# A decoder layer with 32 experts: smaller token units over four column groups, whole-row weight loads and a fixed order of experts

## What is computed

```python
def moe(h, w_router, b_router, w_up, b_up, w_down, b_down):
    B, S, D = h.shape
    t = h.reshape(B * S, D)                       # 256 x 1024
    logits = (t @ w_router + b_router).astype(jnp.float32)
    top_vals, top_idx = lax.top_k(logits, TOP_K)  # 4 of 32
    wts = jax.nn.softmax(top_vals, axis=-1)
    combine = jnp.sum(jax.nn.one_hot(top_idx, N_EXPERTS, dtype=jnp.float32) * wts[..., None],
                      axis=1).astype(t.dtype)
    y = jnp.zeros_like(t)
    for e in range(N_EXPERTS):
        gu = t @ w_up[e] + b_up[e]                # w_up[e]: 1024 x 2048
        glu = jnp.minimum(gu[:, 0::2], SWIGLU_LIMIT)
        lin = jnp.clip(gu[:, 1::2], -SWIGLU_LIMIT, SWIGLU_LIMIT)
        act = glu * jax.nn.sigmoid(SWIGLU_ALPHA * glu) * (lin + 1.0)
        y = y + combine[:, e:e + 1] * (act @ w_down[e] + b_down[e])   # w_down[e]: 1024 x 1024
    return y.reshape(B, S, D)
```

## Time and profile before

| | us |
|---|---|
| median of three runs | 1452.26 |
| span of the profiled execution | 1448.6 |
| TensorE busy | 1330.1 (92%) |
| VectorE busy | 396.9 (27%) |
| ScalarE busy | 217.6 (15%) |
| mean DMA rate over the span | 330 GB/s |
| loads of w_up: 256 of 1 MB, issue to landing | 18.0 |
| loads of w_down: 128 of 1 MB, issue to landing | 18.3 |

### The profile page before, as it was taken

One profiled execution on the slowest core, in us unless ns is written; L12 is line 12 of the kernel. 1 busy time (PEld: TensorE's weight loads), 2 busy tenths in 40 slices (PEclk: granted clock), 3 DMA queues, 4 the chain that ended last, 5 costly groups with the idle time before them and its releaser, 6 DMA issues.

```text
span 1448.6 us, 19177 instructions
## 1 busy us (share of the span) xinstructions
PE 1330.1 (92%) x6949; PEld 534.1 (37%) x6950; DVE 396.9 (27%) x1059; ACT 217.6 (15%) x452; POOL 61.9 (4%) x88
## 2 busy tenths in 40 slices
PE   3999999999997999998888989999998988999997
PEld 0484434444444333332222333333333322333332
DVE  0386980654124211211111111121211112112111
ACT  0200102254012111111111111111111111111110
POOL 4000000002532000000000000000000000000000
PEclk9999999999996999999999999999999999999999
DMA  8936666234644899999999999999999999899997
GB/s 273 368 120 249 215 233 216 73 111 124 196 143 142 339 410 409 410 409 409 410 409 409 410 409 409 371 364 410 409 410 410 409 410 410 324 406 410 410 409 310
DMA packets 143057, 477.40 MB, mean 330 GB/s; under 512 B 9746, under 2 KB 9771, under 8 KB 143036
## 3 DMA queue, kind: packets, MB, share of 16 engines
q1 hardware_dynamic: 138918, 472.28, 84.3%
q0 software_dynamic: 1200, 3.28, 0.9%
q10 hardware_dynamic: 2918, 1.57, 0.4%
HBM read 473.96 MB, written 1.05 MB: 328 GB/s over the span
## 4 chain that ended last, share of the span: by engine, by line
PE 48%; SPq 33%; DMA 11%; issue 4%; ACT 2%; DVE 2%; DVEq 0%
SPq L394 28%; PE bank L1155 13%; PE bank L1392 11%; DMA weights<-in_w_up 10%; PE bank L1408 6%; PE bank L1145 4%; PE bank L1166 3%; PE bank L1113 2%; PE bank L1284 2%; PE bank L1367 2%; PE bank L1359 1%; DMA weights<-in_w_ada 1%; SPq L422 1%; SPq L423 1%; SPq L424 1%
## 5 line engine op out<-in xcount | busy, mean ns | idle before, releaser
L1392 PE MATMUL bank<-weights,buf_d 128*64 128x512 f32 x2176 | 504.7, 601 | 48.1 <-DMA weights<-in_w_up 48.0
L1392 PEld LDWEIGHTS bank<-weights,buf_d 128*64 128x64 f32 x2176 | 145.2, 137 | 379.4 <-issue 244.2
L1408 PE MATMUL bank<-weights,buf_d 128*64 128x512 f32 x1088 | 246.7, 595 | 0.0
L1155 PE MATMUL bank<-weights,buf_d 128*128 128x512 f32 x320 | 140.2, 596 | 0.0
L1408 PEld LDWEIGHTS bank<-weights,buf_d 128*64 128x64 f32 x1088 | 74.1, 136 | 125.6 <-issue 117.6
L816 DVE SCALAR_TENSOR_TENSOR weights<-u_conv,convw,weights 128x256 f32<-128x256 f32 x240 | 96.9, 478 | 0.3
L1082 DVE TENSOR_SCALAR u_conv<-bank 128x256 f32<-128x256 f32 x68 | 28.6, 421 | 246.2 <-PE bank L1392 246.2
L1075 DVE TENSOR_SCALAR u_conv<-iota_s,u_conv 128x128 f32<-128x128 f32 x68 | 20.5, 343 | 270.4 <-PE bank L1392 270.4
L1155 PEld LDWEIGHTS bank<-weights,buf_d 128*128 128x128 f32 x320 | 61.2, 192 | 74.3 <-issue 74.0
L683 ACT COPY buf_d<-bank 128x256 f32<-128x256 f32 x68 | 25.3, 373 | 417.5 <-PE bank L1418 417.5
L687 ACT ACTIVATE u_conv<-u_conv 128x256 f32<-128x256 f32 x34 | 14.2, 417 | 385.8 <-DVE u_conv L1082 385.8
(11 more groups left out here) (293 smaller groups left out, 897.3 us busy)
## 6 DMA issues: line engine op xcount, KB each, us to landing
weights<-in_w_up SPq DMA_DIRECT2D x256, 1024.0 KB, 18.0
weights<-in_w_down SPq DMA_DIRECT2D x128, 1024.0 KB, 18.3
weights<-in_w_in SPq DMA_DIRECT2D x14, 2048.0 KB, 11.2
weights<-in_w_ada SPq DMA_DIRECT2D x12, 2048.0 KB, 15.5
weights<-in_w_conv_out SPq DMA_DIRECT2D x2, 2048.0 KB, 7.8
weights<-in_w_attn_out SPq DMA_DIRECT2D x2, 2048.0 KB, 8.2
weights<-in_w_o SPq DMA_DIRECT2D x2, 2048.0 KB, 11.2
qkT<-modrow POOLq DMA_DIRECT2D x16, 128.0 KB, 3.7
```

The source lines that it names most:

```text
L1155: ins = t.matmul(bank(use)[:, :], lhsT[:, k, P * tt:P * tt + P], blk(n)[:, k, :], start=(k == 0 and bias is None), stop=(k == KD - 1))
L1392: ins = t.matmul(UP[a][SLOTS * i:SLOTS * i + SLOTS, :], xgT[:, k, :], wslot(slot, spare_at)[:, k % 2, NB * i:NB * i + NB], start=False, st ...
L1408: ins = t.matmul(DOWN[SLOTS * i:SLOTS * i + SLOTS, :], actT[:, a, k % 2, SLOTS * (k // 2):SLOTS * (k // 2) + SLOTS], wslot(slot)[:, k % 2, ...
```

## The change

- A unit has up to 32 tokens (SLOTS = 32). The moving operand goes over four column groups of 32 columns each: 32 matmuls in `up` write the four quarters of one bank (UP), 16 in `down` those of another (DOWN).
- An expert is loaded in six chunks of 2 MB (CHUNKS). The four chunks of w_up are 256 whole rows of the matrix each; partition p holds rows 2p and 2p+1, 16 KB in one piece. The two chunks of w_down give a partition two pieces of 8 KB. There are seven slots (NSLOT) in a ring over all 192 chunks of all experts.
- The experts run in fixed order, 0 to 31, each at least once; the program text of a unit stands 32 times, each in a loop over that expert's units. Slots, waits and addresses are constants, but for the number of units used up so far (`unit_ends`), which SP and PE read once for each expert. A chunk is loaded into the slot of the chunk seven before it, when PE has used that one in its expert's last unit (`chunk_used[j]`). The first chunk of expert 1 goes out before the routing, into the slot that nothing else holds.
- Because a partition now holds two neighbouring rows, the stationary operands change: `gather` writes the tokens untransposed (32 x 256 in each of four groups, 24 matmuls with 256 columns), ACT copies them, PE transposes even and odd columns apart, ACT copies again (together with the transposed combine weights).
- One activation step for each unit instead of two, on all 128 partitions.
- The routing arithmetic drops the tables of loads, and counts units of 32 (seven comparisons for an expert in place of three).

The core of the diff:

```diff
-SLOTS = 64
+SLOTS = 32
 UCOLS = 64
+GROUPS = P // SLOTS
+CHUNKS = 6
...
-NSLOT = 12
+NSLOT = 7
...
+        def chunk_slot(e, j):
+            return (CHUNKS * e + j) % NSLOT
+
+        def chunk_landed(e, j):
+            return 16 * ((CHUNKS * e + j) // NSLOT + 1)
+
+        def wslot(e, j):
+            at = chunk_slot(e, j)
+            return W[:, at * BLOCKF:(at + 1) * BLOCKF]
+
+        def up_chunk(e, g):
+            return wslot(e, g).rearrange("p (r n) -> p r n", r=2)
+
+        def down_chunk(e, h):
+            return wslot(e, 4 + h).rearrange("p (g r n) -> p g r n", g=2, r=2)
...
-            def load_unit(e, wait, spare=0):
-                for i in range(NSLOT):
-                    wait(i)
-                    pair = 2 * P * (i % 4)
-                    if i < 8:
-                        col = D * (i // 4)
-                        src = w_up[0, e, pair:pair + 2 * P, col:col + D]
-                    else:
-                        src = w_down[0, e, pair:pair + 2 * P, :]
-                    if not isinstance(e, int):
-                        src = src.rearrange("o a n -> (o a) n")
-                    sp.dma_start(wslot(i, spare), src.rearrange("(k p) n -> p k n", p=P)).then_inc(w_full[i], 16)
...
+            def load_chunk(e, j):
+                if j < 4:
+                    src = w_up[0, e, 2 * P * j:2 * P * j + 2 * P, :].rearrange("(p r) n -> p (r n)", r=2)
+                    dst = wslot(e, j)
                 else:
-                    sp.wait_ge(w_free, before * 9 + 3 * (i // 4) + i % 4 + 1)
-
-
-            e1 = sp.value_load(unit_i[0:1, UCOLS + 1:UCOLS + 2], min_val=0, max_val=EXPERTS - 1)
-            before1 = sp.value_load(unit_i[0:1, 2 * UCOLS + 1:2 * UCOLS + 2], min_val=0, max_val=46)
+                    src = w_down[0, e, NB * (j - 4):NB * (j - 4) + NB, :].rearrange("(g p r) n -> p g (r n)", g=2, r=2)
+                    dst = wslot(e, j).rearrange("p (g n) -> p g n", g=2)
+                sp.dma_start(dst, src).then_inc(w_full[chunk_slot(e, j)], 16)
+
+            for j in range(CHUNKS):
+                sp.wait_ge(*used[len(blocks) - RING + j])
+                load_chunk(0, j)
             sp.wait_ge(h2_high, TT)
             sp.wait_ge(h2_split, 3 * (TT - 1) + 1)
-            load_unit(bass.ds(e1, 1), lambda i: slot_used(i, 16, before1), NSLOT * SLOTF)
-            with sp.Fori(2, loads) as n:
-                e = sp.value_load(unit_i[0:1, bass.ds(n + UCOLS, 1)], min_val=0, max_val=EXPERTS - 1)
-                before = sp.value_load(unit_i[0:1, bass.ds(n + 2 * UCOLS, 1)], min_val=0, max_val=46)
-                before_last = sp.value_load(unit_i[0:1, bass.ds(n + (2 * UCOLS - 1), 1)], min_val=0, max_val=46)
-                spare = sp.value_load(load_spare[0:1, bass.ds(n, 1)], min_val=0, max_val=NSLOT * SLOTF)
-                landed = sp.value_load(load_landed[0:1, bass.ds(n, 1)], min_val=16, max_val=16 * EXPERTS)
-                load_unit(bass.ds(e, 1), lambda i: slot_used(i, landed, before, before_last), spare)
+            full(sp, LG_USE[TT - 1])
+            load_chunk(1, 0)
...
+            for e in range(EXPERTS - 1):
+                end = sp.value_load(unit_ends[0:1, e:e + 1], min_val=e + 1, max_val=UCOLS - 1)
+                for j in range(CHUNKS):
+                    n = CHUNKS * e + j + NSLOT
+                    if n < CHUNKS * EXPERTS:
+                        sp.wait_ge(chunk_used[j], end)
+                        load_chunk(n // CHUNKS, n % CHUNKS)
...
+            s.copy(xg, GX[:, 0:T]).then_inc(xs_ready, 1)
+            act_e.wait_ge(xt_done, 1)
+            s.copy(xgT, GX[:, T:2 * T].rearrange("p (r s) -> p r s", r=2)).then_inc(xc_ready, 1)
...
+                act_e.wait_ge(glu_ready, u + 1)
+                s.activation(sg, glu, ACT.Sigmoid, scale=ALPHA).then_inc(sg_ready, 1)
                 act_e.wait_ge(gathered, u + 2)
-                s.copy(xgT, UP[0][:, :].rearrange("p (k s) -> p k s", k=KD)).then_inc(xg_ready, 1)
-                keep_act(1)
-
-                act_e.wait_ge(ct_done, u + 1)
-                s.copy(Cmb, TR[:, 0:T]).then_inc(cmb_ready, 1)
+                s.copy(xg, GX[:, 0:T]).then_inc(xs_ready, 1)
+                act_e.wait_ge(t_done, u + 1)
+                s.copy(actT, TR[:, 0:T].rearrange("p (r s) -> p r s", r=2)).then_inc(actT_ready, 1)
+                act_e.wait_ge(xt_done, u + 2)
+                s.copy(area_q[:, 0:2 * T], GX[:, :]).then_inc(xc_ready, 1)
...
-                for k in range(KD):
-                    for tt in range(TT):
-                        for i, part in enumerate(h2_parts):
-                            ins = t.matmul(UP[0][:, SLOTS * k:SLOTS * k + SLOTS], part[:, tt, P * k:P * k + P],
-                                           pick[:, tt, :], start=(tt == 0 and i == 0), stop=(tt == TT - 1 and i == 2))
+                for tt in range(TT):
+                    for i, part in enumerate(h2_parts):
+                        for g in range(GROUPS):
+                            ins = t.matmul(GX[SLOTS * g:SLOTS * g + SLOTS, 0:T], pick[:, tt, :], part[:, tt, T * g:T * g + T],
+                                           start=(tt == 0 and i == 0), stop=(tt == TT - 1 and i == 2))
                 ins.then_inc(gathered, 1)
+
+            def transpose_halves(bank_, at, src):
+                for r in range(2):
+                    ins = t.transpose(bank_[:, at + P * r:at + P * r + P], src.rearrange("p (c r) -> p r c", r=2)[:, r, :], ident[:])
+                return ins
...
+            def bias_rows(bank_, groups, col):
+                for n_, g in enumerate(groups):
+                    t.matmul(bank_[SLOTS * g:SLOTS * g + SLOTS, :], sel, ebias[:, col + NB * n_:col + NB * n_ + NB],
+                             start=True, stop=False)
...
+            def unit(e, u):
+                pe.wait_ge(xc_ready, u + 1)
                 pe.wait_ge(sel_ready, u + 1)
-                bias(UP[0], 0)
-                with pe.If(spare == 0):
-                    up_chunks(0, range(2 * SPARE))
-                with pe.Else():
-                    up_chunks(0, range(2 * SPARE), NSLOT * SLOTF)
-                up_chunks(0, range(2 * SPARE, KD)).then_inc(up_done[0], 1)
-                bias(UP[1], D)
-                up_chunks(1, range(KD // 2))
+                bias_rows(UP, range(GROUPS), 0)
+                for j in range(4):
+                    w = up_chunk(e, j)
+                    pe.wait_ge(w_full[chunk_slot(e, j)], chunk_landed(e, j))
+                    for r in range(2):
+                        for g in range(GROUPS):
+                            ins = t.matmul(UP[SLOTS * g:SLOTS * g + SLOTS, :], xgT[:, r, SLOTS * j:SLOTS * j + SLOTS],
+                                           w[:, r, NB * g:NB * g + NB], start=False, stop=(j == 3 and r == 1))
+                    ins.then_inc(chunk_used[j], 1)
 
                 pe.wait_ge(oe_ready, u + 1)
-                pe.wait_ge(cmb_ready, u + 1)
                 combine()
-                up_chunks(1, range(KD // 2, KD)).then_inc(up_done[1], 1)
-                pe.wait_ge(act_ready[0], u + 1)
-                transpose_act(0)
+                bias_rows(DOWN, (0, 2), 2 * D)
                 pe.wait_ge(pick_ready, u + 2)
                 gather()
-                pe.wait_ge(actT_ready[0], u + 1)
-                down(0)
-                pe.wait_ge(act_ready[1], u + 1)
-                transpose_act(1)
+                pe.wait_ge(act_ready, u + 1)
+                transpose_halves(TR, 0, act).then_inc(t_done, 1)
+                pe.wait_ge(xs_ready, u + 2)
+                transpose_halves(GX, T, xg)
                 pe.wait_ge(pickw_ready, u + 1)
-                pe.wait_ge(actT_ready[1], u + 1)
                 for tt in range(TT):
-                    ins = t.transpose(TR[:, P * tt:P * tt + P], pickw[:, tt, :], ident[:])
-                ins.then_inc(ct_done, 1)
-                down(1).then_inc(down_done, 1)
-            pe.wait_ge(cmb_ready, count + 1)
-            pe.wait_ge(oe_ready, count + 1)
+                    ins = t.transpose(GX[:, P * tt:P * tt + P], pickw[:, tt, :], ident[:])
+                ins.then_inc(xt_done, 1)
+
+                pe.wait_ge(actT_ready, u + 1)
+                for h in range(2):
+                    w = down_chunk(e, h)
+                    pe.wait_ge(w_full[chunk_slot(e, 4 + h)], chunk_landed(e, 4 + h))
+                    for g in range(2):
+                        at = SLOTS * (2 * h + g)
+                        for i in range(2):
+                            for r in range(2):
+                                rows = slice(SLOTS * (2 * i + r), SLOTS * (2 * i + r) + SLOTS)
+                                ins = t.matmul(DOWN[rows, :], actT[:, r, at:at + SLOTS], w[:, g, r, NB * i:NB * i + NB],
+                                               start=(r == 1 and h == 0 and g == 0), stop=(h == 1 and g == 1))
+                    ins.then_inc(chunk_used[4 + h], 1)
+
+            begin = 0
+            for e in range(EXPERTS):
```

(6 more changed lines are left out.)

199 lines of the change are left out of this document (53 added, 146 removed).

## The result

The changed kernel takes **1479.51 us** (median of four runs, 1477.41 to 1481.32); the kernel before took 1451.28 beside it (1448.71 to 1455.54). The ratio is **1.019**, with a 95% interval of 1.017 to 1.021: slower by 28 us, and within 1 us of the 1480 forecast. The profiled execution has a span of 1475.5 us.

What follows compares the result with a forecast made beforehand. The prediction took the expert stage to be bound by weight loads, TensorE close behind. Start 468.6, chunks 908.4, empty queues 63.3, clock and restart 24, end 12.0 and 3.7 from span to median gave 1480 us; 8-in-10 range 1442 to 1518.

Steps and rivals of the forecast that it cites:

- The sum: Whole kernel: start 468.6, chunks 908.4, empty queues 63.3, clock and restart 24, end 12.0 give span 1476.3; forecast 1480 us.
- experts 15 and 25: Experts with three and four units: the load queue stands empty for 16.9 and 32.4 us, plus clock and restart.
- ten experts with two units: Refill comes late after each repeated unit: 1.4 us lost at each, plus 2 us each for clock and restart.
- the 24 us for clock and restart: At twelve repeated-unit experts: 2 us each for slow DMA restart and TensorE's low clock together; ends 0 and 80.
- The rate: Expert weight loads: longer rows raise the full-queue DMA rate from 410 to 427 GB/s, 4.91 us a chunk; ends 410 and 435.
- The straight line: Load rate extrapolated from 2 and 4 KB rows: 428 GB/s for 8 KB, 438 for 16 KB, 435 mixed.
- rival A: Expert loads: 435 GB/s and no extra at restarts, so 1439 us; chance 0.32 with the cases up to the forecast.
- rival B: Expert loads: long rows load no faster than 4 KB rows, so 1516 us; chance 0.15 with its surroundings.
- The unit: TensorE's work on up to 32 tokens: 15.5 us with four column groups side by side; 25.8 if no faster than two.
- Rival C: TensorE: four column groups run no faster than two, unit 25.8 us, end about 1690; chance 0.05 together with the low-clock case.
- The empty queue: Expert loads: only an expert's last unit frees slots, so twelve repeated experts lose 63.3 us, against 14.9 before.
- Rival D: TensorE: clock stays at 1.2 GHz throughout, unit about 28 us, about 1590; chance 0.05 together with the slow-column-groups case.

## Why the prediction was right, step by step

**The sum.** Its terms against the trace of the changed kernel:

| term | predicted | measured |
|---|---|---|
| engines move again after the start | 468.6 | 467.3 |
| 185 chunks at the plain rate | 908.4 (427 GB/s) | 911 to 913 (426 to 425) |
| experts 15 and 25 | 49.3 + 4 | 50.0 |
| ten experts with two units | 14 + 20 | 33.4 |
| tail behind the last transfer | 12.0 | 10.1 |
| sum | 1476.3 | 1472 to 1474 of a span of 1475.5 |

Some 2 us of the span stand in no term; the first restart, slow for two microseconds like the others (246 and 213 GB/s at 467 to 469), is about one of them. No term is off by more than 5 us; the rate gave less than forecast, start, sags and tail cost less. The mechanisms held; that the total came within 1 us is luck: 427 GB/s was chosen between 410 and 435, and the 24 us for clock and restart between 0 and 80, and the rate's error of 3 to 5 us met about 7 us the other way from start, sags and tail.

**The rate.** TensorE's start on the first and on the last chunk of w_up of expert 31, each behind a wait for the chunk:

```profile
1441.78 2.74 PE L1346 MATMUL bank<-weights,buf_d 128*32 128x512 f32 x16 [2.75 <-DMA weights<-in_w_up]
...
1456.47 3.56 PE L1346 MATMUL bank<-weights,buf_d 128*32 128x512 f32 x16 [2.97 <-DMA weights<-in_w_up]
```

Three chunks of 2.097 MB in 14.69 us are 428 GB/s for rows of 16 KB, and 15 slots of 8 KB rows gave 421 throughout. The packets of the trace agree: they are whole rows, and one of 16 KB takes 612 ns and one of 8 KB 312 (medians), which is 428 and 420 on 16 engines. The straight line had 438 and 428. So the line bends, as the prediction feared when it took 427 in place of 435, and rival A had too much by 2%. Rows of 4 KB gave 409 in the new slots: rival B is refuted by the changed kernel, and its number for 4 KB rows was right for the rate.

The Trainium skill ("DMA: Bandwidth & Descriptors", "Where 436 GB/s comes from") has a ceiling of 435 GB/s; 428 for rows of 16 KB keeps below it.

**The unit.** 14.8 us in place of 15.5. Up (6.87), down (3.57), combine (1.92), bias (0.44) and gather (0.79) are as worked out; the transposes came to 0.7 with 0.4 of waiting for ACT's copy in place of 1.2, and the 0.9 of gaps was not there. Rival C falls.

The Trainium skill ("TensorE: Matmul & The Clock Gate", Part 3) has 2.38 for three column tiles and 3.07 for four row tiles. Here four column groups give 4.0 over the full array (0.430 us for a record of it, 6.87 / 64 = 0.107 now); the measurement decides.

**The empty queue.** The place, the count and the mechanism were right: one run without repeated units is 82.9 us faster, against 87.3 predicted for the twelve places, and more slots take the ten small sags away. The account of the small ones left one thing out. Expert 8 in single microseconds; TensorE sees the last chunk at L = 703.21:

```profile
703.00:704.00 1.00, 0.79 (x8) 0.29 (x12) 0.00 (x0) 0.00 (x0) 0.00 (x0) 1.00 0.99 410
704.00:705.00 1.00, 1.00 (x16) 0.29 (x12) 0.00 (x0) 0.00 (x0) 0.00 (x0) 1.00 0.46 197
705.00:706.00 1.00, 1.00 (x16) 0.34 (x12) 0.80 (x2) 0.00 (x0) 0.00 (x0) 1.00 0.31 131
706.00:707.00 1.00, 1.00 (x16) 0.37 (x12) 0.70 (x4) 0.00 (x0) 0.00 (x0) 1.00 0.12 49
707.00:708.00 1.00, 1.00 (x16) 0.28 (x11) 0.00 (x0) 0.00 (x0) 0.00 (x0) 1.00 0.00 0
708.00:709.00 1.00, 1.00 (x12) 0.26 (x8) 0.00 (x0) 0.00 (x0) 0.00 (x0) 1.00 1.20 229
709.00:710.00 1.00, 1.00 (x16) 0.37 (x12) 0.00 (x0) 0.00 (x0) 0.00 (x0) 1.00 0.80 262
710.00:711.00 1.00, 1.00 (x16) 0.29 (x12) 0.00 (x0) 0.00 (x0) 0.00 (x0) 1.00 0.99 426
```

SP's row for the refill, on the timeline:

```profile
707.13 3.76 SPq L392 DMA_DIRECT2D weights<-in_w_up  x3
```

The same count at all ten, from the packets and landings in the trace, L being the landing of the expert's last chunk:

| what | predicted | measured | over ten experts |
|---|---|---|---|
| remaining chunk ends, on average over the engines | L + 3.7 | L + 2.0 at expert 8, 4.0 at expert 9, 2.9 to 3.2 at the others | 7 us lost |
| new packets start | L + 5.1 | L + 4.9 to 5.0; 4.6 at expert 9; 6.4 to 6.6 at experts 10, 11 and 27 | 4 us lost at those three, 1 gained at the rest |
| slow restart | in the 2 us | about 1.0 each | 10 us lost |

With the 14 us of the prediction that makes 34, against 33.4 measured. So of the 20 us that it added "for clock and restart", the restart is a half and the clock between a fifth and a quarter; the spread of the engines' ends, a third of it, was missing from the account. Expert 9, where the engines had just been empty together, has the least spread (L + 4.0) and the smallest sag (1.9 us). This is a reading of the trace; no run changed the spread itself.

The clock's part lies at experts 10, 11 and 27. There TensorE had stood 2.6 to 2.8 us waiting for the last chunk and did the half of down in 3.59, 3.62 and 3.37 us in place of 1.92. Expert 10, its row in the chain of waits and the clock in a microsecond of it:

```profile
766.91 3.59 PE bank L1373 x16
...
767.00:768.00 1.00, 1.00 (x8) 0.31 (x12) 0.00 (x0) 0.00 (x0) 0.00 (x0) 0.50 1.00 426
```

The issue came at 772.51, L + 5.6, and the loss was 4.4 us. Two traces with the same loads and the same instructions, in another order within a chunk, show the price at one place: at expert 26 the changed kernel has the half of down in 1.92 us, and the kernel with the groups in pairs has it in 3.61 (for each the row of the chain of waits and the stretch of 20 us; the granted clock of the stretch falls from 1.00 to 0.91).

```profile
1308.27 1.92 PE bank L1373 x16
1300.00:1320.00 20.00, 17.27 (x174) 6.44 (x170) 4.58 (x14) 3.45 (x6) 0.00 (x0) 1.00 0.90 366
...
1309.72 3.61 PE bank L1373 x16
1300.00:1320.00 20.00, 17.14 (x152) 6.02 (x142) 3.28 (x10) 3.03 (x5) 0.00 (x0) 0.91 0.81 328
```

The sag is 2.8 us in the one and 4.6 in the other. So the clock takes 1.5 to 1.8 us at a place where it is low, 5 us of the 33 in the profiled execution, and which places those are differs between these traces.

**The clock in the stage.** 0.86 where TensorE waits for chunks, with 1.00 in the repeated units of experts 15 and 25: the paced unit is so short that a slower one still fits between two chunks. Rival D falls.

The Trainium skill ("TensorE: Matmul & The Clock Gate", "HAM oscillation") describes short bursts between DMA waits as a pattern that throws the clock back. The trace agrees that it does (0.86 over 160 us), and bears out its cost only at a few places: 5 us at the three experts above; with one unit for each expert, 0.85 over 900 us went with the full 425 GB/s. The total stayed at 1480 and did not move towards 1500.

## What to carry to other kernels

Where a stage is bound by its loads, a faster unit is worth nothing by itself; count how often the unit is repeated on the same weights, because that is when no slot comes free, and set the length of the repeats against what the queue holds ahead. Here finer units took 55 us and the new loads gave 25 in the same change; taken apart, the new loads with the old units (1424.6 us), or with half-size chunks and 15 slots (1419.8 us), are ahead of both kernels. Count what is left in the queue from bytes and not from the landing of the last transfer: the landing is that of the slowest engine.

## What the runs showed of the hardware that was not expected

- **The spread of the DMA engines' ends.** When the last 2 MB load of an expert lands, the sixteen engines have on average been through with it for 1.7 to 2.0 us of the 4.92 that the load takes, at eight of the ten experts with two units; 2.9 at expert 8, far from any empty queue, and 0.9 at expert 9, soon after one.
- **A restart depends on the row.** After an empty queue 16 KB rows were back at 426 after two microseconds of 229 and 262; with 4 KB rows the engines counted as full moved 201 to 258 for four. In time lost: 1.0 us (16 KB), 0.9 (8 KB, 1 MB loads), 2.1 (4 KB, 1 MB loads), 2.6 in the kernel before (4 KB).
- **The order of column groups doesn't matter** within a chunk: up took 6.87 to 6.94 us with records of the four groups in turn, in pairs, or four of a group in a row.
- **Rates by row length**, queue full: 378 (2 KB), 409 to 410 (4 KB), 421 (8 KB), 428 (16 KB) GB/s. With 4 and 8 KB both in loads of 1 MB, the row makes the difference.
